# RWKV recurrence: the chunk inverse in 64x64 products, its sums taken in PSUM, and another order of the jobs

## The reference, cut to what matters

```
def step(S, xs):
    r_t, w_t, k_t, v_t, a_t, b_t = xs
    sa = einsum('bhvk,bhk->bhv', S, a_t)
    S = S * w_t + sa[..., None] * b_t + v_t[..., None] * k_t
    return S, einsum('bhvk,bhk->bhv', S, r_t)
```

## Time and profile before

| | us |
|---|---|
| median of three runs | 3524.1 |
| lowest, highest | 3513.17, 3540.83 |
| the profiled execution | 3541.05 |
| its span | 3539.3 |
| TensorE busy | 2984.3 (84%) |
| VectorE busy | 1374.2 (39%) |
| ScalarE busy | 509.7 (14%) |
| mean granted clock | 0.882 |

### The profile page before, as it was taken

One profiled execution on the slowest core, in us unless ns is written; L12 is line 12 of the kernel. 1 busy time (PEld: TensorE's weight loads), 2 busy tenths in 40 slices (PEclk: granted clock), 3 DMA queues, 4 the chain that ended last, 5 costly groups with the idle time before them and its releaser, 6 DMA issues. The chain is left out here.

```text
span 3539.3 us, 78591 instructions
## 1 busy us (share of the span) xinstructions
PE 2984.3 (84%) x35105; PEld 1728.2 (49%) x35105; DVE 1374.2 (39%) x2442; ACT 509.7 (14%) x1254; POOL 396.6 (11%) x488
## 2 busy tenths in 40 slices
PE   5899999996766878778877469995999999999993
PEld 1566676664555666666666234452333332333331
DVE  1676766673343344444443311224213222223123
ACT  2100000002231222222222211111001000000001
POOL 0100000000353222222221100000000000000000
PEclk8899999998686687887787689997999999999997
DMA  9575555552430000000000757785999999999997
GB/s 412 179 219 179 182 201 195 194 189 103 120 95 19 21 4 25 25 25 24 23 3 16 281 194 292 289 334 216 383 400 413 396 397 401 395 412 411 397 419 301
DMA packets 224700, 777.26 MB, mean 220 GB/s; under 512 B 55362, under 2 KB 119577, under 8 KB 155826
## 3 DMA queue, kind: packets, MB, share of 16 engines
q1 hardware_dynamic: 212818, 712.28, 52.2%
q0 software_dynamic: 11248, 60.87, 5.7%
q10 hardware_dynamic: 368, 0.10, 0.0%
HBM read 711.00 MB, written 62.18 MB: 218 GB/s over the span
## 5 line engine op out<-in xcount | busy, mean ns | idle before, releaser
L2135 PE MATMUL ex_ps<-experts_ring,ex_xe 128*32 128x512 f32 (+1 forms) x4608 | 678.0, 601 | 48.6 <-DMA experts_ring<-in_w_up 26.8
L2137 PE MATMUL ex_ps<-experts_ring,ex_xe 128*32 128x512 f32 (+1 forms) x1536 | 677.5, 601 | 0.0
L2135 PEld LDWEIGHTS ex_ps<-experts_ring,ex_xe 128*32 128x32 f32 (+1 forms) x4608 | 213.8, 107 | 498.1 <-issue 480.7
L476 DVE SCALAR_TENSOR_TENSOR pj_macc<-pj_mring,head_cond_t,pj_macc 128x1024 f32<-128x1024 f32 x240 | 296.9, 1278 | 183.5 <-DMA pj_mring<-in_w_ada 183.5
L2150 PE MATMUL ex_ps<-experts_ring,ex_hidt 128*32 128x512 f32 (+1 forms) x2304 | 334.6, 595 | 6.9 <-DVE ex_hidt L2217 6.9
L2152 PE MATMUL ex_ps<-experts_ring,ex_hidt 128*32 128x512 f32 (+1 forms) x768 | 334.1, 595 | 0.0
L549 PE MATMUL pj_ps<-head_hT,head_ring_in 128*128 128x320 f32 x1104 | 313.4, 437 | 5.9 <-DVE head_hT L449 3.5
L1933 PE MATMUL om_ps<-experts_ring,om_ot 128*128 128x512 f32 x640 | 287.6, 611 | 15.1 <-DMA om_ot<-scratch_o 15.1
L549 PEld LDWEIGHTS pj_ps<-head_hT,head_ring_in 128*128 128x128 f32 x1104 | 211.3, 192 | 96.6 <-DVE head_hT L449 6.3
L2239 DVE SCALAR_TENSOR_TENSOR ex_hid<-ex_hid,ex_gcol,ex_ps 80x512 f32<-80x512 f32 x16 | 11.9, 744 | 594.1 <-ACT ex_hid L2182 594.1
L2150 PEld LDWEIGHTS ex_ps<-experts_ring,ex_hidt 128*32 128x32 f32 (+1 forms) x2304 | 106.7, 106 | 226.0 <-issue 218.2
(11 more groups left out here) (359 smaller groups left out, 3999.7 us busy)
## 6 DMA issues: line engine op xcount, KB each, us to landing
experts_ring<-in_w_gate SPq DMA_DIRECT2D x128, 1024.0 KB, 19.4
experts_ring<-in_w_up SPq DMA_DIRECT2D x128, 1024.0 KB, 22.2
experts_ring<-in_w_down SPq DMA_DIRECT2D x128, 1024.0 KB, 20.9
experts_ring<-in_w_out SPq DMA_DIRECT2D x68, 1024.0 KB, 7.1
pj_mring<-in_w_ada SPq DMA_DIRECT2D x64, 1024.0 KB, 9.2
head_ring_in<-in_w_in SPq DMA_DIRECT2D x23, 2048.0 KB
ada_ring<-in_w_ada SPq DMA_DIRECT2D x16, 2048.0 KB, 20.7
scratch_z<-pj_stage POOLq DMA_DIRECT2D x19, 640.0 KB, 8.3
```

The lines of the kernel that those rows point to most:

```text
L476: a = nc.vector.scalar_tensor_tensor(acc, w, scalar, acc, ALU.mult, ALU.add)
L2135: pe.matmul(ps[rows, bank, :], xe[:, k, rows], cols, start=(k == 0), stop=(k == KD - 1))
L2137: mm = pe.matmul(ps[96:96 + rows.stop - rows.start, bank, :], xe[:, k, rows], up[:, g1], start=(k == 0), stop=(k == KD - 1))
```

## The change

The products of the inverse run in 64x64 tiles. For that three operands are 64 columns wide: `near` has the diagonal 32x32 blocks of the scores and zeros beside them, `far` the off-diagonal ones; ScalarE makes both from `sc` (`halve`). `xm` is 64 wide, and the masks `kept` (made by POOL in the set-up) put zeros beside its blocks. `w` and `a` are two products of 64 columns each instead of one of 128.

The sum into `tt` at levels 0 to 3 is made in PSUM: an identity product writes the old `tt` into the bank, and the `d` products accumulate on it. VectorE transposes `tm` from the bank, and ScalarE copies `tt` out of it after that. The mask of the last level moves from ScalarE's side (a plain copy) to VectorE.

The order of a unit is another: `w` and `a` come first, two stages of the chain follow each `sc`, one follows each `x` and each `d`; `scan` comes after the second `sc`, and `removal`, the exponentials and the `pad` operations each come earlier. `COST` is gone. The first `pw` of a unit's chain no longer waits for the inverse, its first `u` does. The counters `ecp` and `spread` are one.

```diff
--- before.py
+++ after.py
@@ -1085,30 +1085,21 @@
 
     def plan(u):
 
-        fr = front_jobs(u + 1) + [None] * 5
-        vt = [("vt", b, u) for b in range(2)] if u % 2 == 0 else [None] * 2
-        more = u + 1 < NU
-        items = [("sc", 0, u), fr[0], ("sc", 1, u), fr[1], ("sc", 2, u), fr[2], ("sc", 3, u), fr[3], ("sc", 4, u)]
-        items += ["scan"] if more else []
-        fill = [("bk", 0, u), ("bk", 1, u), ("bk", 2, u), fr[4], vt[0], vt[1]]
+        w0, w1, a0, a1, s0 = front_jobs(u + 1) or [None] * 5
+        vt0, vt1 = [("vt", b, u) if u % 2 == 0 else None for b in range(2)]
+        fill = {0: [("bk", 0, u), ("bk", 1, u)], 1: [("bk", 2, u), s0], 2: [vt0, vt1]}
+        then = {(0, 1): ["removal"], (2, 0): ["exp_in"], (2, 1): ["exp_inv"], (3, 0): ["exp_ex", "decay", "pad_b"], (3, 1): ["pad_k"], (4, 0): ["pad_a"]}
+        items = [w0, a0, w1, a1]
+        for b in range(NCK // 2):
+            items += [("sc", b, u)] + (["scan"] if b == 1 else []) + ["slot", "slot"]
         for lv in range(LAST_LV + 1):
-            for b in range(2):
-                items += (["turn%d" % b] if lv == 0 else []) + [("x", b, lv, u)]
-            if lv < 3:
-                items.append(fill[2 * lv])
-            if more and lv == 2:
-                items.append("removal")
-            for b in range(2):
-                items.append(("d", b, lv, u))
-                if more and lv == 3:
-                    items.append(("exp_in", "exp_inv")[b])
-                if more and lv == 4:
-                    items += (["pad_b"], ["pad_k", "pad_a"])[b]
-            if lv < 3:
-                items.append(fill[2 * lv + 1])
-            if more and lv == 3:
-                items += ["exp_ex", "decay"]
-        return [i for i in items if i is not None]
+            for k, kind in enumerate(("x", "d")):
+                for b in range(2):
+                    items += (["turn%d" % b] if (lv, kind) == (0, "x") else []) + [(kind, b, lv, u), "slot"]
+                    items += [fill[lv][k]] if lv in fill and b == 0 else []
+                items += then.get((lv, k), [])
+        skip = () if u + 1 < NU else ("scan", "removal", "exp_in", "exp_inv", "exp_ex", "decay", "pad_b", "pad_k", "pad_a")
+        return [i for i in items if i is not None and i not in skip]
 
     def chain(v, i0, i1):
         return [("seq", v, i, s) for i in range(i0, i1) for s in ("pw", "u", "z")] if 0 <= v < NU else []
@@ -1119,17 +1110,16 @@
         old, new = chain(u - 2, BC, NCK), chain(u - 1, 0, BC)
         return [s for pair in itertools.zip_longest(old, new) for s in pair if s is not None]
 
-    COST = {"sc": 9, "w": 6, "a": 6, "s0": 2, "bk": 9, "vt": 6, "x": 7, "d": 7}
-
     def timeline(u):
 
         items, seq = plan(u) if u < NU else [], sequence(u)
-        total = sum(COST[i[0]] for i in items if not isinstance(i, str))
-        out, spent, placed = [], 0, 0
+        slots, out, seen, placed = items.count("slot"), [], 0, 0
         for i in items:
-            out.append(i)
-            spent += 0 if isinstance(i, str) else COST[i[0]]
-            while placed < len(seq) and (placed + 1) * total <= spent * len(seq):
+            if i != "slot":
+                out.append(i)
+                continue
+            seen += 1
+            while placed * slots < seen * len(seq):
                 out.append(seq[placed])
                 placed += 1
         return out + seq[placed:]
...
@@ -1271,8 +1263,12 @@
             for g, rows in enumerate(GROUPS):
                 for h in range(2):
                     ch.link(nc.gpsimd.memset(half[rows, h:h + 1], 1.0 if h == g % 2 else 0.0))
-            for h in range(2):
-                ch.link(nc.gpsimd.tensor_scalar(first[:, h, :], join[:, 0, :], half[:, h:h + 1], None, ALU.mult))
+            for i in range(5):
+                for h in range(2):
+                    ch.link(nc.gpsimd.tensor_scalar(kept[:, i, h, :], join[:, i, :], half[:, h:h + 1], None, ALU.mult))
+            ch.link(nc.gpsimd.memset(kept[:, 5:7], 0.0))
+            for d in range(2):
+                ch.link(nc.gpsimd.tensor_scalar(kept[:, 5 + d, d, :], join[:, 5, :], half[:, 1 - d:2 - d], None, ALU.mult))
             assert ch.n == MADE, ch.n
             for s in (*o_ev, *z_ev, *u_ev, osum_done, o_out, fo_out):
                 pool.sem_inc(s, 1)
...
@@ -1379,6 +1376,8 @@
                     pe.wait_ge(turned, 10 * u + 2 * lv + b + 1)
                 elif kind == "d":
                     before.append(("x", b, key[2], u))
+                    if 0 < key[2]:
+                        before.append(("d", b, key[2] - 1, u))
                 emptied(before)
                 if kind in ("w", "a", "s0"):
                     d, p = u % 2, u // 2
@@ -1388,7 +1387,8 @@
                         mm = heads(bank[:, 0:DH], sin[:, p % 2, d, :], eye[:], True, True)
                     else:
                         rows = HEADS[0 if kind == "w" else 1]
-                        mm = pe.matmul(bank[:, 0:HALF], wa2[rows, p % 2, d, :], xwa[rows, b * HALF:(b + 1) * HALF], start=True, stop=True)
+                        for cols in HEADS:
+                            mm = pe.matmul(bank[cols, 0:HALF], wa2[rows, p % 2, d, cols], xwa[rows, b * HALF:(b + 1) * HALF], start=True, stop=True)
                 elif kind == "vt":
                     pe.wait_ge(loads, (u // 2 + 1) * NLOAD)
                     for i in range(BC):
@@ -1407,18 +1407,16 @@
                             mm = heads(bank[:, (2 * i + j) * P:(2 * i + j + 1) * P], bk[:, u % 2, j * NCK + c, :],
                                        aq[:, u % 4, c].rearrange("p i t -> p (i t)"), True, True)
                 else:
-                    last = key[2] == LAST_LV
+                    if kind == "x" and key[2] in (0, LAST_LV):
+                        pe.wait_ge(halved, 3 * u + (3 if key[2] else b + 1))
+                    lt = far if key[2] == LAST_LV else near
+                    summed = kind == "d" and key[2] < LAST_LV
+                    if summed:
+                        heads(bank[:, 0:BC * HB], eye[:], chunks(tt, b).rearrange("p c k -> p (c k)"), True, False, skip_group_check=True)
                     for i in range(BC):
                         c = BC * b + i
-                        out = bank[:, i * HB:(i + 1) * HB]
-                        for g, rows in enumerate(GROUPS):
-                            at = GROUPS[g ^ 1] if last else rows
-                            if kind == "x":
-                                h = (g + 1) % 2 if last else g % 2
-                                lhs, rhs = sc[rows, u % NS, c, 0, HB * h:HB * h + HB], tm[rows, c, :]
-                            else:
-                                lhs, rhs = xm[rows, c, :], tt[rows, c, :]
-                            mm = pe.matmul(out[at], lhs, rhs, start=True, stop=True)
+                        lhs, rhs = (lt[:, c, :], tm[:, c, :]) if kind == "x" else (xm[:, c, :], tt[:, c, :])
+                        mm = heads(bank[:, i * HB:(i + 1) * HB], lhs, rhs, not summed, True, skip_group_check=True)
                 mm.then_inc(job, 1)
 
             def stage(v, i, s):
@@ -1431,8 +1429,7 @@
                 vk = vtok[:, v // 2 % 2, c, :]
                 if s == "pw":
                     if i == 0:
-                        emptied([("x", 1, LAST_LV, v), ("d", 1, LAST_LV, v)])
-                        pe.wait_ge(spread, 2 * v + 2)
+                        emptied([("bk", 2, v), ("vt", 1, v - v % 2), ("sc", NCK // 2 - 1, v)])
                     pe.wait_ge(z_ev[k], q + 1)
                     pe.wait_ge(o_ev[k], q + 1)
                     pe.wait_ge(u_ev[k], q + 1)
@@ -1448,6 +1445,9 @@
                     heads(ov, st[:, k, :], aq[:, v % 4, c, 1, :], False, False, skip_group_check=True)
                 elif s == "u":
                     pe.wait_ge(w_ev[k], q + 1)
+                    if i == 0:
+                        emptied([("d", 1, LAST_LV, v)])
+                        pe.wait_ge(spread, 3 * v + 3)
                     heads(uv, tw[:, n, c, :], wsb[:, k, :], True, True).then_inc(u_done[k], 1)
                 else:
                     pe.wait_ge(u_ev[k], q + 2)
@@ -1490,9 +1490,18 @@
                 elif kind == "bk":
                     m = min(8, 2 * NCK - 8 * b)
                     a = nc.scalar.copy(bktok[:, u % NS, 8 * b:8 * b + m, :].rearrange("p c k -> p (c k)"), bank[:, 0:m * DH])
-                else:
-                    a = nc.scalar.copy(chunks(xm, b).rearrange("p c k -> p (c k)"), bank[:, 0:BC * HB])
+                elif kind == "d":
+                    act.wait_ge(turned, 10 * u + 2 * key[2] + b + 3)
+                    a = nc.scalar.copy(chunks(tt, b).rearrange("p c k -> p (c k)"), bank[:, 0:BC * HB])
                 a.then_inc(act_ev, 1)
+
+            def halve(u, dst, c0, c1, other):
+
+                act.wait_ge(dve_ev, RANK[G["sc", (c1 - 1) // 2, u]])
+                for h in range(2):
+                    lt = sc[:, u % NS, c0:c1, 0, HB * h:HB * h + HB]
```

(45 more changed lines are left out.)

7 lines of the change are left out of this document (3 added, 4 removed).

## The result

The changed kernel takes 3305.7 us (median of four runs, 3300.7 to 3310.8), the kernel before 3527.4: a ratio of 0.937, interval 0.933 to 0.941. Forecast were 3383 and a range from 3310.

What follows compares the result with a forecast made beforehand. TensorE was taken to wait for its program in the level phase, with cold clock and product length partly hidden. 14 steady units x 9.8 us = 137, first two units 8, head +4: total -141, so 3383 us; range 3310 to 3465.

Steps and rivals of the forecast that it cites:

- the clock: TensorE's granted clock: its shortfall shrinks in proportion to idle time, 0.22 to 0.12, so 0.88 instead of 0.78.
- Idle time: TensorE's idle time in a steady unit: from 10.9 to 6.0 us after all changes in waits.
- The first two units: Units with no chain or half of one, mostly waiting for their own results: 8 us less in all.
- Program fetch sets the level phase: Level phase: TensorE waits for code, 3.7 us per 256 instructions; with fewer records gaps go, -3.0 of 3.5 us a unit.
- Rival 1: Level phase: issue gaps stay, from another cause or slower blocks; 4.0 us less a unit, 3464 us; chance 0.15.
- The aq wait: Wait for rw_aq before the first score product: filled by w and a, pad_a earlier; -2.5 us a unit.
- The scan: Moved from behind sc 4 to behind sc 1, it makes pw wait for z: +1.9 us a unit.
- Level 0: Waits at x 0 and x 1 for near: about 1.1 and 1.5 us, 2.6 instead of 3.3, -0.7 a unit.
- Products: TensorE at full clock: x 0.585 us, d 0.875 (0.585 last level), w and a 2.4; work 33.5 us a unit, 32.8 before.
- rival 2: Small products: weight and moving columns add up, 0.87 us a job instead of 0.585; 3475 us; chance 0.06.
- Rival 3: Level phase: new products get the low clock throughout, +10.3 us a unit, 3672 us; chance 0.05.
- Rival 4: Waits of scan and level 0 hide behind each other, clock 0.96: 15.5 us less a unit, 3299 us; chance 0.13.

Runs made afterwards that it cites:

- scan_late: The changed kernel with the scan behind sc 4, as before the change, instead of behind the second score job; ratio 0.953, 3367 us.
- half_products: The kernel before, own order and 32x32 tiles, second head's small products replaced by two zero-weight products: 992 matmul records a unit instead of 1312; ratio 0.967, 3426 us.
- order_small_tiles: The kernel before (32x32 products, add on VectorE, w and a of 128 columns) in the new order of jobs; ratio 0.967, 3425 us.
- idle_spread2: The changed kernel with three ScalarE copies of 2560 columns a unit, ahead of the tt copies of half 0 at levels 1 to 3; ratio 0.944, 3328 us.

## Why the prediction was right in kind and wrong in size

- **The step that failed is the clock.** "I let the shortfall shrink with the idle time" gave 0.88; it is 0.98. Even with the idle time that came out, 4.3 us, the rule gives 0.22 x 4.3 / 10.9 = 0.09, so 0.91. At 33.5 us of work that is 33.5 / 0.88 - 33.5 / 0.98 = 3.9 us a unit, 50 us over the 13 units of the window. The profiled executions differ by 235 us, 94 more than forecast, so this is over half of the miss. What the runs put in the rule's place is partial: the clock follows how idle time stands as well as its sum (scan_late, 64 us for 13 of idle time). The changed kernel's 4.3 us, none over 1.4 in one piece, cost nearly no clock.
- **Idle time** came to 4.3 instead of 6.0: 1.7 us a unit, 22 us over the window. Of it 0.5 are gaps that I had kept, 0.5 the scan, 0.1 level 0, and 0.6 the waits of other kinds. Those, 1.6 us before, were two thirds gaps too: they stood not only before the small products but before others, and all of them went.
- **The first two units** gave 33 us where I took 8: from 109 us at a clock of 0.61 to 77 at 0.86. 19 of them are idle time (38 before, 19 after), the rest goes with the clock. No run takes this apart.
- **Program fetch sets the level phase**: right, and shown from both sides. half_products lost the gaps in the old tiles, order_small_tiles kept them in the new order. The rule of the Trainium skill ("Runtime: NRT & Kernel Launch", section Instruction fetch mechanics), by which fetching is hidden, does not hold here. Rival 1, by which the gaps would stay, is out: 0.3 us of them are left in the window.
- **The aq wait**: right, -2.5; 0.3 us of waiting for rw_sg is new in its place.
- **The scan**: +1.9 forecast, 1.4 measured. **Level 0**: 1.1 and 1.5 forecast, 1.04 and 1.41 measured. What I did not see is that the scan's new place replaces a piece of 3.3 by ones of 1.4 and 1.0: left behind sc 4 it would have cost 0.8 us of idle time more, not 1.2 less.
- **Products**: x 0.585 forecast, 0.55 measured; d 0.875, and 0.83 measured. Weight columns set the pace, with no sum of weights and moving columns: rival 2 is out. w and a 2.4 forecast, 1.4 measured in every second unit and 2.3 in the others; that they overlap I had missed. The sum of the work held partly by luck: TensorE is not idle for 34.1 us a unit, which at 0.98 is 33.4, beside 33.5, although these terms came out 1.3 lower. The first pair of products behind each small job takes 0.15 us instead of 0.12, 0.6 in all; the rest of what the other terms lacked is not attributed.
- **Rival 3**, the low clock in the level phase: it is 1.00 there. **Rival 4** was near in its numbers, a unit of 38.4, clock 0.96, 3299, but only half for its reason: the clock stayed up, while the scan's wait and those of level 0 did not hide behind each other. I gave it 0.13 and a range that stopped above its time.

## What to carry to other kernels

Where a TensorE stream of small products shows idle time ended by nothing, count the instructions between two such gaps. If the count is always the same, save records (fewer, wider products) rather than array time. And don't price idle time by its sum alone. Where it came in one piece of 3.3 us with another behind it, 0.8 us more of it cost 3.4 us a unit; 4.3 us in pieces of at most 1.4 cost nearly no clock; from 5.5 us on, short pieces cost clock as well.

## What the runs showed of the hardware

- TensorE's program came in blocks of 16 KB on queue q8, and the gaps stood a whole number of blocks of some 127 matmuls with their weight loads, 256 instructions, apart. In the window of the kernel before no two packets came closer than 3.4 us. 1312 records a unit with as many weight loads left 4.6 to 5.4 us of gaps, 992 left at most 1, 952 none.
- A product with 64 weight columns takes 0.055 us a pass for 32 moving columns and 0.058 for 64.
- Products of 320 columns on rows 0 to 63 and 64 to 127 overlapped: four jobs in 1.4 us, where one by itself took 0.74.
- The granted clock fell from 0.98 to 0.90 by 0.8 us more idle time a unit, as it came with one piece of 3.3 us. In idle_spread2 the same waits went with a clock of 1.00 and then of 0.90. How the chip decides on it is left open.
